# Feed-forwards: two 256-column products that share a weight become one of 512 columns

## The chip, the cores and the metric

One core of one Trainium2 chip runs the whole program. The metric is the device time of one execution in microseconds (us). Five engines work from queues of their own and meet at semaphores: TensorE (PE in the profile, its weight loads PEld), VectorE (DVE), ScalarE (ACT), GpSimd (POOL) and SyncE (SP), which here issues the loads of the weights.

## The reference

Three blocks in sequence act on 256 tokens of width 1024. Each has feed-forwards of width 2816 or other wide layers, and between them stand different mixers (attention, a convolution, a product-key memory). Eight feed-forwards of one kind are what the change touches:

```
def _swiglu(x, w_gate, w_up, w_down):
    return (jax.nn.silu(x @ w_gate) * (x @ w_up)) @ w_down
...
x = x + 0.5 * _swiglu(_rmsnorm(x, ffn1_norm[l]), ffn1_w_gate[l], ffn1_w_up[l], ffn1_w_down[l])
```

All of it is in fp32, with inputs and weights in fp32.

## The kernel before

**Two parts of each number.** A weight and an input are each held as a high part, rounded to the format fp32r, and a low part, the rest of the subtraction, in fp32r too. A product of the two is made of three matmuls into the same PSUM columns, in `product`: high weight by high input (L655), high weight by low input (L656), low weight by high input (L657). Each of them has 128 x 128 weights and 256 columns (the tokens), and each loads its weights itself: the high weight is loaded twice.

**Slabs.** Weights come in slabs of 1 MB (128 partitions x 2048 numbers), 16 products each, in one order for the whole program. SyncE loads slab m into a ring of 4 buffers, when slab m-4 has been used (`slab_done`). ScalarE's `round_slab` copies it to one of 3 buffers of high parts (L1427), when slab m-3 has been used, since that slab lies in the same buffer. VectorE's `rest_slab` subtracts (L1916) and puts the low part over the slab itself. Then `slab_rest` lets TensorE begin it. In all feed-forwards but their first steps ScalarE and VectorE have two slabs ready beyond the one on TensorE.

**A feed-forward** (`ffn` of the three engines) has 33 slabs. Slabs 0 to 21 are *ups*: up f gives 128 gate and 128 up columns of the hidden layer, in one of four pairs of PSUM banks (columns 0 to 255 of each bank; a bank holds 512). VectorE multiplies both by the norm's factor (`up_scaled`, L2015: PSUM to SBUF, 128x512), ScalarE applies Silu to the gate (L1509), VectorE multiplies gate and up (L2008), ScalarE copies the high part of the result (L1504) and VectorE subtracts for the low part (L2001). These five stand one tick apart: in tick t an engine rounds a slab, then does its later step for up t-2, then for t-1, then for t. Slabs 22 to 32 are *downs*, r = 0 to 10: each holds two of the 22 rows of weights, for 8 output chunks of 128 that gather in all 8 PSUM banks over all downs. In the last down (r = 10) the chunks end pair by pair, and VectorE adds half of each to x (L2028, `finish`) before the next stage takes its input from x.

At the start of a feed-forward, ups 0 and 1 run interleaved, TensorE sums the squares of x (L726, L727), and VectorE and ScalarE make the factor from the sums (a square root, then L1939, a reciprocal) before L2015 of up 0.

**Order.** Every engine's instructions stand in the order in which its `ffn` issues them. VectorE has, after its last tick, ten `rest_slab` in a row, then the adds to x. ScalarE has eleven `round_slab`. The tenth of VectorE's and of ScalarE's belongs to slab 33, the first of the next stage, which uses the buffer of high parts that slab 30 (down r = 8) holds.

## Time and profile before

| what | us |
|---|---|
| median of three runs | 4007.13 |
| lowest and highest of them | 4005.62, 4008.4 |
| span of the profiled execution, first to last instruction | 4004.4 |

The profiled execution's own device time is not listed apart from the three runs; they lie 1.2 to 4.0 us above its span, the median 2.7. TensorE is busy for 98% of the span, VectorE for 68%, ScalarE for 50%. How to read it: a matmul's duration (276 ns) is the time from its start to its modelled end, and matmuls overlap; what one costs is the distance from one start to the next. "PEclk" is the granted clock of TensorE as a share of 2.4 GHz; 0.50 is 1.2 GHz.

### The profile page before, as it was taken

What the parts mean: (1) busy time and instruction counts of PE and PEld (TensorE: products, weight loads), DVE (VectorE), ACT (ScalarE), POOL (GpSimd) and SP (SyncE); (2) the same over time, 40 slices, a digit from 0 to 9 for tenths busy, and PEclk for the clock granted to TensorE, in tenths of its full rate; (3) what the DMA queues carried; (4) which work ended last, traced back from release to release, by engine and by line L of the source; (5) the groups of instructions that cost most, each with busy time, mean ns of one, the idle gap of its engine ahead of it and who ended that gap; (6) DMA issues with size and microseconds to landing.
All of it is one profiled execution on the core that took longest, in us unless ns stands there. A gap on an engine that the chain in (4) does not pass through costs nothing.

```text
span 4004.4 us, 78708 instructions
## 1 busy us (share of the span) xinstructions
PE 3909.7 (98%) x34150; PEld 3793.3 (95%) x34150; DVE 2736.3 (68%) x4071; ACT 1987.8 (50%) x2620; POOL 212.2 (5%) x277
## 2 busy tenths in 40 slices
PE   8999999999999999999999999999999999999999
PEld 8979999889998999999997999999998899999999
DVE  6566665666655656567555799956756699974855
ACT  5445444454544545465435545754444544764443
POOL 0011000110002000010023000000000000000000
PEclk9999999999999999999998999999999999999999
DMA  6534555345555455534550455456654455455754
GB/s 237 192 115 151 192 190 190 133 148 195 181 194 182 160 199 184 195 133 173 191 204 34 159 194 181 177 199 233 229 196 153 158 177 193 175 182 202 265 199 158
DMA packets 114791, 720.78 MB, mean 180 GB/s; under 512 B 13328, under 2 KB 13664, under 8 KB 32784
## 3 DMA queue, kind: packets, MB, share of 16 engines
q1 hardware_dynamic: 90144, 652.25, 45.9%
q10 hardware_dynamic: 19200, 37.01, 2.5%
q0 software_dynamic: 5104, 26.49, 1.9%
q8 instruction: 270, 4.42, 0.4%
q14 instruction: 73, 0.60, 0.0%
HBM read 692.48 MB, written 23.22 MB: 179 GB/s over the span
## 4 chain that ended last, share of the span: by engine, by line
PE 87%; DVE 7%; ACT 4%; issue 1%; POOL 0%; DMA 0%; ACTq 0%; DVEq 0%; POOLq 0%
PE psum L655 26%; PE psum L657 26%; PE psum L656 26%; PE psum L1408 3%; DVE slab_low L1916 2%; ACT slab_high L1427 2%; DVE h_parts L2219 1%; PE psum L1065 1%; PE psum L1048 1%; PE psum L875 1%; PE psum L1078 1%; ACT room L1670 1%; DVE room L2248 0%; DVE room L2253 0%; PE psum L1349 0%
## 5 line engine op out<-in xcount | busy, mean ns | idle before, releaser
L1916 DVE TENSOR_TENSOR slab_low<-slab,slab_high 128x2048 fp32r<-128x2048 f32 x622 | 1423.2, 2289 | 738.8 <-ACT slab_high L1427 736.6
L655 PE MATMUL psum<-h_parts,slab_high 128*128 128x256 f32 x5632 | 1578.2, 280 | 28.9 <-DVE h_parts L2219 18.6
L1427 ACT ACTIVATE slab_high<-slab 128x2048 fp32r<-128x2048 f32 x622 | 1189.3, 1912 | 785.4 <-PE psum L657 721.1
L656 PE MATMUL psum<-h_parts,slab_high 128*128 128x256 f32 x5632 | 1556.5, 276 | 0.0
L657 PE MATMUL psum<-h_parts,slab_low 128*128 128x256 f32 x5632 | 1556.1, 276 | 0.0
L655 PEld LDWEIGHTS psum<-h_parts,slab_high 128*128 128x128 f32 x5632 | 1063.5, 189 | 48.8 <-issue 24.0
L655 PE MATMUL psum<-hidden_parts,slab_high 128*128 128x256 f32 x3840 | 1063.5, 277 | 11.4 <-DVE hidden_parts L2166 4.8
L656 PEld LDWEIGHTS psum<-h_parts,slab_high 128*128 128x128 f32 x5632 | 1063.5, 189 | 2.4 <-issue 2.2
L657 PEld LDWEIGHTS psum<-h_parts,slab_low 128*128 128x128 f32 x5632 | 1062.8, 189 | 0.0
L656 PE MATMUL psum<-hidden_parts,slab_high 128*128 128x256 f32 x3840 | 1058.0, 276 | 0.0
L657 PE MATMUL psum<-hidden_parts,slab_low 128*128 128x256 f32 x3840 | 1058.0, 276 | 0.0
L655 PEld LDWEIGHTS psum<-hidden_parts,slab_high 128*128 128x128 f32 x3840 | 722.0, 188 | 21.6 <-issue 12.9
L656 PEld LDWEIGHTS psum<-hidden_parts,slab_high 128*128 128x128 f32 x3840 | 722.2, 188 | 0.0
L657 PEld LDWEIGHTS psum<-hidden_parts,slab_low 128*128 128x128 f32 x3840 | 722.0, 188 | 0.0
L1889 ACT ACTIVATE hidden_parts<-room 128x512 fp32r<-128x512 f32 x128 | 80.9, 632 | 303.7 <-PE psum L657 294.7
L1880 ACT ACTIVATE room<-psum 128x512 f32<-128x512 f32 x128 | 76.5, 598 | 283.1 <-PE psum L657 283.1
L2598 DVE TENSOR_TENSOR hidden_parts<-room,hidden_parts 128x512 fp32r<-128x512 f32 x128 | 88.2, 690 | 135.1 <-ACT hidden_parts L1889 134.9
L2015 DVE TENSOR_TENSOR room<-psum,room 128x512 f32<-128x512 f32 x176 | 121.3, 689 | 62.8 <-PE psum L657 61.7
L2569 DVE TENSOR_SCALAR room<-consts,room 128x128 f32<-128x128 f32 x512 | 136.4, 339 | 0.0
L1408 PE MATMUL psum<-room 128*128 128x128 f32 x1024 | 124.5, 275 | 0.0
L1670 ACT ACTIVATE room<-room 128x128 f32<-128x128 f32 (+1 forms) x160 | 71.4, 448 | 105.6 <-DVE room L2253 78.6
L1408 PEld LDWEIGHTS psum<-room 128*128 128x128 f32 x1024 | 119.4, 191 | 0.0
(346 smaller groups left out, 3326.0 us busy)
## 6 DMA issues: line engine op xcount, KB each, us to landing
slab<-in_up SPq DMA_DIRECT2D x176, 1024.0 KB, 4.8
slab<-in_keys_up SPq DMA_DIRECT2D x128, 1024.0 KB, 4.8
slab<-in_keys_down SPq DMA_DIRECT2D x128, 1024.0 KB, 4.8
slab<-in_down SPq DMA_DIRECT2D x88, 1024.0 KB, 4.8
slab<-in_w_in SPq DMA_DIRECT2D x16, 1024.0 KB, 4.8
slab<-in_wq SPq DMA_DIRECT2D x16, 1024.0 KB, 4.8
peer_gates<-room ACTq DMA_DIRECT2D x64, 256.0 KB, 2.3
room<-peer_gates ACTq DMA_DIRECT2D x64, 256.0 KB, 5.4
```

Source lines behind the costliest of these rows:

```text
L655: nc.tensor.matmul(out, lhs[0], rhs[0], start=first, stop=False, **options)
L656: nc.tensor.matmul(out, lhs[0], rhs[1], start=False, stop=False, **options)
L657: return nc.tensor.matmul(out, lhs[1], rhs[0], start=False, stop=last, **options)
L1408: mm = nc.tensor.matmul(bank[:, t, :], v.firsts[:, b % 2, t, :], v.seconds[b % 2][:, t, :], start=True, stop=True)
L1427: nc.scalar.activation(k.high[m % PARTS][:, 0:width], k.slabs[m % RING][:, 0:width], ACT.Copy).then_inc(k.rounded.up())
L1670: ex = nc.scalar.activation(row, row, ACT.Exp, bias=small[:, e:e + 1], accum_out=small[:, 4 + e:5 + e])
L1880: nc.scalar.activation(v.hidden[:, at:at + 2, :], k.banks[4 + r % 2].rearrange("p (e t) -> p e t", e=2), ACT.Gelu_apprx_tanh).then_inc(k.a ...
L1889: nc.scalar.activation(k.hidden[:, at:at + 2, 0, :], v.hidden[:, place:place + 2, :], ACT.Copy).then_inc(k.hidden_rounded.up())
L1916: nc.vector.tensor_tensor(k.low[m % RING][:, 0:width], k.slabs[m % RING][:, 0:width], k.high[m % PARTS][:, 0:width], ALU.subtract).then_in ...
L2015: nc.vector.tensor_tensor(both, k.bank_pairs[(f + k.first_pair) % 4][:, :, 0:T], v.rstd.unsqueeze(1).to_broadcast([P, 2, T]), ALU.mult).th ...
L2569: hot = nc.vector.tensor_scalar(v.seconds[b % 2][:, t, :], iota, v.slots[:, 1, t0 + t:t0 + t + 1], v.slots[:, 2, t0 + t:t0 + t + 1], ALU.i ...
L2598: nc.vector.tensor_tensor(k.hidden[:, at:at + 2, 1, :], v.hidden[:, place:place + 2, :], k.hidden[:, at:at + 2, 0, :], ALU.subtract).then_ ...
```

## The change

An up's product now consists of two matmuls (`wide_product`): high weight by both input parts, which lie next to each other, 512 columns into a whole PSUM bank; and low weight by high input, 256 columns into its first half. The second half then holds the sums with the low input part, which has to be added by another engine. In an up ScalarE copies the second halves of the pair to SBUF and VectorE adds the first halves to them (`up_summed`); the scaling by the norm's factor is then an instruction of its own, SBUF to SBUF. In downs r = 0 to 8 the products are wide as well; after r = 8 VectorE adds half of each second half to x (four instructions, `lows_added`), and r = 9 and 10 use the three-matmul product into the first halves. Down r = 8 works four chunks at a time, and down r = 9 waits for the add of a pair of banks before it first writes that pair.

```diff
+WIDE_DOWNS = 9
...
+    def wide_product(self, bank, lhs, rhs, first, last):
+        nc = self.k.nc
+        nc.tensor.matmul(bank, lhs[0], rhs, start=first, stop=last, skip_group_check=True)
+        return nc.tensor.matmul(bank[:, 0:T], lhs[1], rhs[:, 0, :], start=False, stop=last, skip_group_check=True)
...
             if f >= 4:
-                nc.tensor.wait_ge(k.up_scaled.sem, k.up_scaled.at(f - 3))
+                nc.tensor.wait_ge(k.up_summed.sem, k.up_summed.at(f - 3))
...
             if f >= 2:
                 for a in range(2):
                     for c in range(DC):
-                        mm = self.product(pair[:, a], [part[:, a, c, :] for part in w], (k.h[:, c, 0, :], k.h[:, c, 1, :]), c == 0, c == DC - 1)
+                        mm = self.wide_product(pair[:, a], [part[:, a, c, :] for part in w], k.h[:, c], c == 0, c == DC - 1)
...
+            if r >= WIDE_DOWNS - 1:
+                nc.tensor.wait_ge(k.hidden_ready.sem, k.hidden_ready.at(2 * r + 2))
+                for half, e, n in itertools.product(range(2), range(2), range(DC // 2)):
+                    c, f = 4 * half + n, 2 * r + e
+                    cols = slice(e * D + c * P, e * D + (c + 1) * P)
+                    if r == WIDE_DOWNS - 1:
+                        mm = self.wide_product(k.banks[c], (high[:, cols], low[:, cols]), k.hidden[:, f], False, e == 1)
+                        if half == 0 and e == 1 and n == DC // 2 - 1:
+                            mm.then_inc(k.lows_done.up())
+                        continue
+                    if r == WIDE_DOWNS and e == 0 and n % 2 == 0:
+                        nc.tensor.wait_ge(k.lows_added.sem, k.lows_added.at(c // 2 + 1))
+                    mm = self.product(k.banks[c][:, 0:T], (high[:, cols], low[:, cols]), (k.hidden[:, f, 0, :], k.hidden[:, f, 1, :]), False, False, skip_group_check=True)
...
+            if tick < FC:
+                f = tick
+                nc.scalar.wait_ge(k.slab_done.sem, k.slab_done.at(f + 1))
+                nc.scalar.activation(v.both[:, f % 2], k.bank_pairs[(f + k.first_pair) % 4][:, :, T:2 * T], ACT.Copy).then_inc(k.up_copied.up())
...
-                nc.vector.wait_ge(k.slab_done.sem, k.slab_done.at(f + 1))
-                if f >= 2:
-                    nc.vector.wait_ge(k.multiplied.sem, k.multiplied.at(f - 1))
-                nc.vector.tensor_tensor(both, k.bank_pairs[(f + k.first_pair) % 4][:, :, 0:T], v.rstd.unsqueeze(1).to_broadcast([P, 2, T]),
-                                        ALU.mult).then_inc(k.up_scaled.up())
+                nc.vector.wait_ge(k.up_copied.sem, k.up_copied.at(f + 1))
+                nc.vector.tensor_tensor(both, k.bank_pairs[(f + k.first_pair) % 4][:, :, 0:T], both, ALU.add).then_inc(k.up_summed.up())
+                nc.vector.wait_ge(k.up_summed.sem, k.up_summed.at(f + 1))
+                nc.vector.tensor_tensor(both, both, v.rstd.unsqueeze(1).to_broadcast([P, 2, T]), ALU.mult).then_inc(k.up_scaled.up())
         for r in range(FC // 2 - 1):
             self.rest_slab()
+        for j in range(DC // 2):
+            if j == 0:
+                nc.vector.wait_ge(k.lows_done.sem, k.lows_done.at(1))
+            if j == 2:
+                nc.vector.wait_ge(k.slab_done.sem, k.slab_done.at(FC + WIDE_DOWNS))
+            both = k.x[:, 2 * j:2 * j + 2, :]
+            nc.vector.scalar_tensor_tensor(out=both, in0=k.bank_pairs[j][:, :, T:2 * T], scalar=0.5, in1=both,
+                                           op0=ALU.mult, op1=ALU.add).then_inc(k.lows_added.up())
```

On TensorE, where the first feed-forward passes from down r = 8 (its last row in `slab_high0`) to r = 9 (`slab_high1`), before the change:

```order
L655 MATMUL psum<-hidden_parts_66,slab_high0_57 128x256
L656 MATMUL psum<-hidden_parts_66,slab_high0_57 128x256
L657 MATMUL psum<-hidden_parts_66,slab_low2_55 128x256
L655 MATMUL psum<-hidden_parts_66,slab_high1_58 128x256 [waits hidden_ready,slab_rest]
L656 MATMUL psum<-hidden_parts_66,slab_high1_58 128x256
L657 MATMUL psum<-hidden_parts_66,slab_low3_56 128x256
```

The same place after the change:

```order
L664 MATMUL psum<-hidden_parts_66,slab_high0_57 128x512
L665 MATMUL psum<-hidden_parts_66,slab_low2_55 128x256
L657 MATMUL psum<-hidden_parts_66,slab_high1_58 128x256 [waits lows_added,hidden_ready,slab_rest]
L658 MATMUL psum<-hidden_parts_66,slab_high1_58 128x256
L659 MATMUL psum<-hidden_parts_66,slab_low3_56 128x256
```

A product of down r = 8 has two matmuls in place of three, and the first matmul of r = 9 waits for `lows_added` too.

On VectorE, at the end of the same feed-forward (the last two of its ten `rest_slab`, slabs 32 and 33, and what follows; x is the running sum, `h_parts` the next stage's input), before the change:

```order
L1916 TENSOR_TENSOR slab_low0_53<-slab0_49,slab_high2_59 128x2048 [waits slab_rounded]
L1916 TENSOR_TENSOR slab_low1_54<-slab1_50,slab_high0_57 128x2048 [waits slab_rounded]
L2028 SCALAR_TENSOR_TENSOR x_63<-psum,x_63 128x512 [waits pair_done] x2
L2219 SCALAR_TENSOR_TENSOR h_parts_60<-x_63,vectors_61,h_parts_60 128x256 [waits h_rounded] x2
L2028 SCALAR_TENSOR_TENSOR x_63<-psum,x_63 128x512 [waits pair_done]
```

The same place after the change:

```order
L1942 TENSOR_TENSOR slab_low0_53<-slab0_49,slab_high2_59 128x2048 [waits slab_rounded]
L1942 TENSOR_TENSOR slab_low1_54<-slab1_50,slab_high0_57 128x2048 [waits slab_rounded]
L2050 SCALAR_TENSOR_TENSOR x_63<-psum,x_63 128x512 [waits lows_done]
L2050 SCALAR_TENSOR_TENSOR x_63<-psum,x_63 128x512
L2050 SCALAR_TENSOR_TENSOR x_63<-psum,x_63 128x512 [waits slab_done]
L2050 SCALAR_TENSOR_TENSOR x_63<-psum,x_63 128x512
L2062 SCALAR_TENSOR_TENSOR x_63<-psum,x_63 128x512 [waits pair_done,lows_added]
```

The four new adds (L2050) stand behind the low part of slab 33, whose high part goes into the buffer that r = 8 reads.

On VectorE, one tick in the midst of the first feed-forward's ups, before the change:

```order
L1916 TENSOR_TENSOR slab_low2_55<-slab2_51,slab_high1_58 128x2048 [waits slab_rounded]
L2001 TENSOR_TENSOR hidden_parts_66<-room_65,hidden_parts_66 128x256 [waits hidden_rounded]
L2008 TENSOR_TENSOR room_65<-room_65 128x256 [waits hidden_ready,gated]
L2015 TENSOR_TENSOR room_65<-psum,room_65 128x512 [waits multiplied,slab_done]
L1916 TENSOR_TENSOR slab_low3_56<-slab3_52,slab_high2_59 128x2048 [waits slab_rounded]
```

A tick after the change:

```order
L1942 TENSOR_TENSOR slab_low1_54<-slab1_50,slab_high0_57 128x2048 [waits slab_rounded]
L2027 TENSOR_TENSOR hidden_parts_66<-room_65,hidden_parts_66 128x256 [waits hidden_rounded]
L2034 TENSOR_TENSOR room_65<-room_65 128x256 [waits hidden_ready,gated]
L2039 TENSOR_TENSOR room_65<-psum,room_65 128x512 [waits up_copied]
L2041 TENSOR_TENSOR room_65<-room_65 128x512 [waits up_summed]
L1942 TENSOR_TENSOR slab_low2_55<-slab2_51,slab_high1_58 128x2048 [waits slab_rounded]
```

One instruction over PSUM has become one over PSUM that waits for ScalarE, and one over SBUF.

## Rows read from the trace of the kernel before

**Rows 1.** The page: busy time of each engine; shares of the last-ending chain.

```profile
PE 3909.7 (98%) x34150; PEld 3793.3 (95%) x34150; DVE 2736.3 (68%) x4071; ACT 1987.8 (50%) x2620; POOL 212.2 (5%) x277
PE 87%; DVE 7%; ACT 4%; issue 1%; POOL 0%; DMA 0%; ACTq 0%; DVEq 0%; POOLq 0%
```

**Rows 2.** Timeline, ScalarE, late downs of feed-forward 1: start us, us, instruction [idle before].

```profile
182.26 1.92 ACT L1427 ACTIVATE slab_high<-slab 128x2048 fp32r<-128x2048 f32 x1 [3.52 <-PE psum L657]
187.70 1.92 ACT L1427 ACTIVATE slab_high<-slab 128x2048 fp32r<-128x2048 f32 x1 [3.52 <-PE psum L657]
```

**Rows 3.** Timeline, TensorE in an up: the first and last of 28 matmuls.

```profile
59.95 0.28 PE L655 MATMUL psum<-h_parts,slab_high 128*128 128x256 f32 x1
...
63.01 0.28 PE L655 MATMUL psum<-h_parts,slab_high 128*128 128x256 f32 x1
```

**Rows 4.** Timeline, TensorE, matmuls of 128 columns: first and last of ten.

```profile
227.35 0.27 PE L657 MATMUL psum<-slab_high,h_parts 128*128 128x128 f32 x1
...
228.35 0.28 PE L657 MATMUL psum<-slab_high,h_parts 128*128 128x128 f32 x1
```

**Rows 5.** Timeline, TensorE, plain fp32: first and thirteenth of 256 columns; one of 512.

```profile
2012.17 0.59 PE L1180 MATMUL psum<-room 128*128 128x256 f32 x2
...
2017.36 0.59 PE L1180 MATMUL psum<-room 128*128 128x256 f32 x2
...
2092.89 1.02 PE L1235 MATMUL psum<-room,consts 128*128 128x512 f32 x2
2093.74 0.51 PE L1256 MATMUL psum<-consts,room 128*128 128x16 f32 x4
```

**Rows 6.** Groups by line and form: ScalarE from PSUM, VectorE within SBUF (count | busy, mean ns).

```profile
L1880 ACT ACTIVATE room<-psum 128x512 f32<-128x512 f32 x128 | 76.5, 598 | 283.1 <-PE psum L657 283.1
L2598 DVE TENSOR_TENSOR hidden_parts<-room,hidden_parts 128x512 fp32r<-128x512 f32 x128 | 88.2, 690 | 135.1 <-ACT hidden_parts L1889 134.9
```

**Rows 7.** Timeline, VectorE and ScalarE, a tick in the ups.

```profile
105.16 0.42 DVE L2008 TENSOR_TENSOR room<-room 128x256 f32<-128x256 f32 x1
106.05 0.69 DVE L2015 TENSOR_TENSOR room<-psum,room 128x512 f32<-128x512 f32 x1 [0.46 <-PE psum L657]
108.06 2.29 DVE L1916 TENSOR_TENSOR slab_low<-slab,slab_high 128x2048 fp32r<-128x2048 f32 x1 [1.32 <-ACT slab_high L1427]
...
106.10 1.92 ACT L1427 ACTIVATE slab_high<-slab 128x2048 fp32r<-128x2048 f32 x1 [2.91 <-PE psum L657]
```

**Rows 8.** Timeline, VectorE and TensorE, start of feed-forward 6.

```profile
1345.56 1.75 DVE L1939 RECIPROCAL room<-room 128x256 f32<-128x256 f32 x1 [0.48 <-ACT room L1451]
1347.34 0.69 DVE L2015 TENSOR_TENSOR room<-psum,room 128x512 f32<-128x512 f32 x1
1347.95 2.28 DVE L1916 TENSOR_TENSOR slab_low<-slab,slab_high 128x2048 fp32r<-128x2048 f32 x1
...
1350.29 0.39 PE L655 MATMUL psum<-h_parts,slab_high 128*128 128x256 f32 x1 [0.20 <-DVE slab_low L1916]
```

**Rows 9.** Timeline, VectorE, late downs of feed-forward 1 (the tenth low part, then x).

```profile
189.66 2.29 DVE L1916 TENSOR_TENSOR slab_low<-slab,slab_high 128x2048 fp32r<-128x2048 f32 x1 [3.15 <-ACT slab_high L1427]
194.44 0.69 DVE L2028 SCALAR_TENSOR_TENSOR x<-psum,x 128x512 f32<-128x512 f32 x1 [2.49 <-PE psum L657]
```

**Rows 10.** Windows of 2 us around TensorE's longest late wait: us, PE, PEld, DVE, ACT, POOL, PEclk, DMA.

```profile
1302.00:1304.00 2.00, 0.28 (x2) 0.00 (x0) 1.20 (x2) 1.21 (x2) 0.00 (x0) 1.00 0.00 0
1304.00:1306.00 2.00, 0.00 (x0) 0.00 (x0) 1.74 (x3) 1.02 (x2) 0.00 (x0) 0.83 0.00 0
1310.00:1312.00 2.00, 2.00 (x12) 2.00 (x11) 0.00 (x0) 0.00 (x0) 0.00 (x0) 0.50 0.00 0
```

**Rows 11.** Timeline, TensorE behind two waits: first matmul and first at full pace.

```profile
1307.12 0.55 PE L655 MATMUL psum<-hidden_parts,slab_high 128*128 128x256 f32 x1 [4.84 <-DVE hidden_parts L2166]
...
1312.17 0.28 PE L657 MATMUL psum<-hidden_parts,slab_low 128*128 128x256 f32 x1
...
3069.74 0.38 PE L655 MATMUL psum<-h_parts,slab_high 128*128 128x256 f32 x1
...
3073.50 0.28 PE L655 MATMUL psum<-h_parts,slab_high 128*128 128x256 f32 x1
```

More of the change, by code:

```diff
@@ L231, in __init__ @@
         self.up_scaled, self.gated, self.multiplied = signal("up_scaled"), signal("gated"), signal("multiplied")
+        self.up_copied, self.up_summed, self.lows_added, self.lows_done = (signal(n) for n in ("up_copied", "up_summed", "lows_added", "lows_done"))
         self.pair_done = signal("pair_done")
@@ L691, in ffn @@
             at = (f + k.first_pair) % 4
-            pair = k.bank_pairs[at][:, :, 0:T]
+            pair = k.bank_pairs[at]
             if f >= 4:
-                nc.tensor.wait_ge(k.up_scaled.sem, k.up_scaled.at(f - 3))
+                nc.tensor.wait_ge(k.up_summed.sem, k.up_summed.at(f - 3))
             elif f >= 2 or k.first_pair < 2:
@@ L703, in ffn @@
                 firsts, lag = [], FIRST_LAG if first else DC if k.before == "ffn" else 2
-                pairs = [k.bank_pairs[g + k.first_pair][:, :, 0:T] for g in range(2)]
+                pairs = [k.bank_pairs[g + k.first_pair] for g in range(2)]
                 for step in range(DC + lag):
@@ L714, in ffn @@
                         for a in range(2):
-                            mm = self.product(pairs[g][:, a], [part[:, a, c, :] for part in firsts[g]], (k.h[:, c, 0, :], k.h[:, c, 1, :]), c == 0, c == DC - 1)
+                            mm = self.wide_product(pairs[g][:, a], [part[:, a, c, :] for part in firsts[g]], k.h[:, c], c == 0, c == DC - 1)
                         if c == DC - 1:
@@ L733, in ffn @@
             if f == 5 and first:
-                nc.tensor.wait_ge(k.up_scaled.sem, k.up_scaled.at(4))
+                nc.tensor.wait_ge(k.up_summed.sem, k.up_summed.at(4))
                 self.bias_lines()
@@ L742, in ffn @@
                     mm = self.product(k.banks[2 * j + c][:, 0:T], (high[:, cols], low[:, cols]),
-                                      (k.hidden[:, 2 * r + e, 0, :], k.hidden[:, 2 * r + e, 1, :]), False, e == 1)
+                                      (k.hidden[:, 2 * r + e, 0, :], k.hidden[:, 2 * r + e, 1, :]), False, e == 1, skip_group_check=True)
                     if e == 1 and c == 1 and j < 3:
@@ L747, in ffn @@
                 break
+            if r >= WIDE_DOWNS - 1:
[11 more added lines that the diff above has]
+                    mm = self.product(k.banks[c][:, 0:T], (high[:, cols], low[:, cols]), (k.hidden[:, f, 0, :], k.hidden[:, f, 1, :]), False, False, skip_group_check=True)
+                mm.then_inc(k.slab_done.up())
+                continue
             for e in range(2):
@@ L754, in ffn @@
                     if f == 0 and n % 2 == 0:
-                        nc.tensor.wait_ge(k.up_scaled.sem, k.up_scaled.at(FC - 3 + n // 2))
+                        nc.tensor.wait_ge(k.up_summed.sem, k.up_summed.at(FC - 3 + n // 2))
                     cols = slice(e * D + c * P, e * D + (c + 1) * P)
-                    mm = self.product(k.banks[c][:, 0:T], (high[:, cols], low[:, cols]), (k.hidden[:, f, 0, :], k.hidden[:, f, 1, :]),
-                                      f == 0, False)
+                    mm = self.wide_product(k.banks[c], (high[:, cols], low[:, cols]), k.hidden[:, f], f == 0, False)
             mm.then_inc(k.slab_done.up())
@@ L2011, in ffn @@
                 both = v.both[:, f % 2]
[L2012 to L2016 removed]
+                nc.vector.wait_ge(k.up_copied.sem, k.up_copied.at(f + 1))
+                nc.vector.tensor_tensor(both, k.bank_pairs[(f + k.first_pair) % 4][:, :, 0:T], both, ALU.add).then_inc(k.up_summed.up())
+                nc.vector.wait_ge(k.up_summed.sem, k.up_summed.at(f + 1))
+                nc.vector.tensor_tensor(both, both, v.rstd.unsqueeze(1).to_broadcast([P, 2, T]), ALU.mult).then_inc(k.up_scaled.up())
         for r in range(FC // 2 - 1):
             self.rest_slab()
+        for j in range(DC // 2):
[6 more added lines that the diff above has]
+                                           op0=ALU.mult, op1=ALU.add).then_inc(k.lows_added.up())
         self.owed = True
+        nc.vector.wait_ge(k.lows_added.sem, k.lows_added.at(DC // 2))
         pair_done, all_done = [k.pair_done.at(j + 1) for j in range(3)], k.slab_done.at(FC + FC // 2)
```

## Prediction

> **What bounds the kernel now.** I began with the page's busy times and its chain of waits: TensorE is busy for 98% of the span and holds 87% of the chain [rows 1], so the question is what one product costs on TensorE, and whether anything new makes it wait. The busy share does not answer the first, since matmul durations overlap; the pace does. In the downs, ScalarE starts a slab each time TensorE has finished one, at 182.26 and 187.70: 5.44 us for a slab of 48 matmuls, 113.3 ns each [rows 2]. I went through these starts in the ups and downs of all eight feed-forwards: nearly every distance is 5.44. Single starts agree: 27 distances in 3.06 us are 113.3 ns [rows 3]. A product of three is 340.0 ns.
>
> What makes up the 113.3? With 128 columns, half the streaming, nine distances take 1.00 us: 111.1 ns [rows 4]. So columns are not what sets it there; each of these matmuls loads 128 x 128 weights, and I read 111 ns as the least distance between two loads. Streaming alone shows in plain fp32. There twelve steps of 256 columns take 5.19 us, 432.5 ns a step, and a step of 512 columns takes 0.85 us, twice that [rows 5]; each step has two records, and 432.5 is four times 108.1, so I read four passes of 256 / 2.4 GHz = 106.7 ns with little on top. The matmuls of the feed-forward thus lie where the two limits meet: 107 to 108 ns of streaming, 111 of loading, 113.3 together.
>
> **TensorE's gain.** A wide product has one matmul of 512 columns and one of 256, two loads in place of three. The load for the second lies beside 213.3 ns of streaming and is hidden; the load for the next product lies beside 256 columns as now. So it costs 512 columns at the pace of the fp32 passes, 2 x 108.1 = 216.2, plus 113.3, together 329.5; with a load per matmul I allow half a nanosecond more and take 330, a gain of 10.0 ns. The bounds: if the 6.6 ns above streaming come with each matmul (113.3 - 106.7), one of them is saved, 6.7 ns; if nothing but streaming counted, the product would take 213.3 + 107.5 = 320.8, a gain of 19.2. I choose near the fp32 rows since they show 512 columns without a surcharge. There are 8 x (22 + 9) x 16 = 3968 wide products: **-39.7 us** (bounds -26.6 and -76.2).
>
> The Trainium skill, in TensorE: Matmul & The Clock Gate, section Back-to-back issue gap, gives an isolated matmul of N columns N / 2.4 + 2.5 ns. By that a product would fall from 327.5 to 325.0 only, 9.9 us in all, and the sum below would be 4061.6. The row has 113.3 where this formula has 109.2, so it leaves out the load; the sum goes by the rows.
>
> **The ups' extra work, at nothing.** Per up ScalarE gets a PSUM copy of 128x512, 0.60 us by its like, and VectorE one more pass over 128x512 in SBUF, 0.69 by its like [rows 6]. Call the end of a slab 0, as ScalarE and VectorE see it in [rows 7] (106.10, 106.05). Now: copy to 0.65, rounding of the next slab to 2.55; VectorE adds to 1.3, scales to 1.95, idles until 2.55, makes the low part to 4.8, then its two steps of 0.35 to 5.5. The next slab ends at 16 x 0.330 = 5.28, its copy at 5.93: VectorE still waits some 0.4 us in each tick. And the low part so made is for the slab after the next two, needed 5.5 us later than it is done. A bank pair comes free 0.6 us later than now, three slabs ahead of its use; for the first down's last pair, whose adding ends 1.6 us into 1.98 us of other products, 0.4 us is left. What hides all this is VectorE's idle time; if a tick were longer than the slab, each 0.1 us would cost 176 x 0.1 = 17.6 us.
>
> **The start of a feed-forward.** Here VectorE has no idle time. The reciprocal ends at 1347.31, L2015 of up 0 follows at 1347.34, the low part at 1347.95, and TensorE waits for it until 1350.29 [rows 8]. The copy on ScalarE hides beside the reciprocal, but the scaling now puts 0.6 us ahead of the low part; and the 16 products that TensorE runs meanwhile end 0.16 us sooner. I found such a wait in seven of the eight feed-forwards: 7 x 0.76 = 5.3, with a little for the eighth **+6 us** (3 to 9).
>
> **The new wait at down 9.** TensorE may not begin r = 9 before VectorE has added the first pair's low halves. On VectorE that add stands behind the low part of slab 33, this behind ScalarE's rounding of slab 33, and this waits until slab 30, which is r = 8 itself, is done. So none of the chain can run beside r = 8. Its length stands in the trace: ScalarE starts at 187.70 [rows 2], VectorE's low part at 189.66, 1.96 later; it takes 2.29, of which the next instruction waits 2.21; an add of x from PSUM takes 0.69 [rows 9]. That is 4.86 us from ScalarE's start. TensorE's next start would have been 0.26 before it (187.44 in the timeline), and the restart costs about 0.05 and a load of 0.12: 5.3 us of nothing on TensorE. Behind it the second pair's add comes 0.6 later, in time for TensorE. Nothing is paid back: slabs 31 and 32 were ready anyway, and the next stage waits for x, which is late by the same. Eight times: **+42.4 us**.
>
> **The clock behind the wait.** After the wait of 4.84 us the granted clock had fallen from 1.00 to 0.50, 1.2 GHz, while TensorE was idle, and stayed there [rows 10]. Matmuls then stand 213 ns apart; from the restart at 1307.12 to the first at full pace at 1312.17 there are 23, in 5.05 us where 2.61 would have done: 2.44 lost. A shorter break ended in 18 at this pace, 3.76 us for 2.04: 1.72 lost [rows 11]. I take 2.0: 8 x 2.0 = **+16.0 us** (0 if it stayed up, 19 at the longer). The Trainium skill, same page, section Why this matters for your kernels, warns that idle gaps between bursts of matmuls send the array back to half rate; by that rule the change pays beyond its idle time, and the trace agrees, with 0.50 at 1310.
>
> **Sum.** 4004.4 (the profiled span) - 39.7 + 6 + 42.4 + 16.0 = 4029.1; the median of the runs lies 2.7 above that span, so **4031.8**, 0.6% slower.
>
> **The rivals.**
> *Streaming only (faster).* If the second load too can be hidden beside the 512 columns, the gain is 76.2: 3995.3. For it: both loads, 222 ns, are shorter than the stream. Against: 113.3 lies above both limits, so a load does not start before its predecessor's matmul. Costs of 64.4 us over 3968 products make 16.2 ns the gain from which the change is faster.
> *The clock holds.* Terms as above without 16.0: 4015.8. Against: in [rows 10] it fell during a shorter wait than the new one.
> *Nothing is saved.* If the surplus grows with the columns (226.6 + 113.3 = 340), only costs are left, 42.4 + 16.0 + 4.2 (the scaling alone at the seven starts): 4069.7. Against: 512 fp32 columns at exactly twice 256.
> *VectorE becomes the bound in the ups.* A tick of 5.4 us in place of 5.28 would give 21 us more, 4053. Against: 0.4 us of room.
>
> **How the numbers follow.** The forecast has 0.68, nothing saved 0.09, the clock holds 0.08, VectorE bound 0.08, streaming only 0.07. The forecast's own range: at a gain of 13 ns (51.6), a start of 3 and stalls of 6.6 each, 4011; at 6.7 ns, 9 and 7.6, 4050. That leaves out about 2 in 10 with the cases beyond, so 4010 to 4052 is the range. What a measurement can tell from no change is about 0.2%, 8 us: faster means below 3999 (streaming only, and a rest: 0.08), same up to 4015 (half of the clock's case and the forecast's low end: 0.12), slower 0.80.
>
> **What the profile would show.** Right: slabs every 5.28 us in the ups; before each r = 9 an idle TensorE of about 5 us, released by VectorE's L2050, and a clock of 0.50 behind it; VectorE idle before L2039 in the ups. Wrong: a slab time of 5.44 (nothing saved) or 5.13 (streaming only); waits of TensorE for `up_summed` or low parts in the middle of the ups (VectorE bound); or r = 9 starting within a microsecond of r = 8, which would mean that I misread the order on VectorE.

## The result, and the profile after

The changed kernel takes 4120.01 us (median of four runs, 4119.01 to 4121.45), the kernel before 4006.38 beside it (4004.87 to 4008.4): a ratio of 1.0281, 95% interval 1.0267 to 1.0296. It is 114 us slower; 25 were predicted. The profiled execution has a span of 4118.8 us, 114.4 more than before.

The page, busy times and chain, to be read against [rows 1]:

```profile
PE 3976.0 (97%) x30182; PEld 3673.8 (89%) x30182; DVE 2875.2 (70%) x4279; ACT 2073.3 (50%) x2796; POOL 215.5 (5%) x277
PE 86%; DVE 8%; ACT 4%; issue 1%; DMA 0%; POOL 0%; ACTq 0%; DVEq 0%; POOLq 0%
```

TensorE has 3968 instructions fewer and is busy 66 us longer. Its pace, in the timeline of the changed kernel in an up, a wide product and the first of the next:

```profile
80.24 0.40 PE L664 MATMUL psum<-h_parts,slab_high 128*128 128x512 f32 x1
80.48 0.28 PE L665 MATMUL psum<-h_parts,slab_low 128*128 128x256 f32 x1
80.60 0.40 PE L664 MATMUL psum<-h_parts,slab_high 128*128 128x512 f32 x1
```

From one wide product to the next is 0.36 us: the 512 columns take 0.24 and the 256 behind them 0.12 (medians over all the ups 235 and 118 ns). The slabs say it more finely, as in [rows 2]; the timeline of ScalarE in the changed kernel, the first and the fourth of four starts:

```profile
81.65 1.91 ACT L1449 ACTIVATE slab_high<-slab 128x2048 fp32r<-128x2048 f32 x1
...
98.61 1.91 ACT L1449 ACTIVATE slab_high<-slab 128x2048 fp32r<-128x2048 f32 x1
```

16.96 us for three slabs, 5.65 each where 5.28 was forecast, are 353.3 ns a product, where three matmuls took 340.0: a loss of 13.3 ns, 3968 times, **52.8 us**, instead of a gain of 39.7.

The wait at down 9. First the changed kernel's groups of waits (us in total, times, longest), then its timelines of VectorE and TensorE in feed-forward 1:

```profile
PE psum L657 <- DVE x L2050: 41.4, 8, 5.8
```

```profile
196.22 2.29 DVE L1942 TENSOR_TENSOR slab_low<-slab,slab_high 128x2048 fp32r<-128x2048 f32 x1 [3.35 <-ACT slab_high L1449]
198.43 2.48 DVE L2050 SCALAR_TENSOR_TENSOR x<-psum,x 128x512 f32<-128x512 f32 x4
...
199.26 0.55 PE L657 MATMUL psum<-hidden_parts,slab_high 128*128 128x256 f32 x1 [5.08 <-DVE x L2050]
```

Eight waits, 41.4 us in all. And the clock behind this one (windows of 2 us, columns as in [rows 10]):

```profile
194.00:196.00 2.00, 0.18 (x2) 0.00 (x0) 0.00 (x0) 1.72 (x1) 0.00 (x0) 1.00 0.36 57
196.00:198.00 2.00, 0.00 (x0) 0.00 (x0) 1.78 (x1) 0.19 (x1) 0.00 (x0) 0.75 0.92 381
198.00:200.00 2.00, 0.74 (x3) 0.77 (x4) 2.00 (x4) 0.00 (x0) 0.00 (x0) 0.50 0.21 86
...
204.00:206.00 2.00, 2.00 (x20) 2.00 (x19) 0.00 (x0) 0.00 (x0) 0.00 (x0) 1.00 0.00 0
```

The granted clock falls to 0.50 in the wait and stays there for 3.1 to 5.9 us behind each of the eight restarts. Counted as at [rows 11], the matmuls up to the first at full pace lost 1.49 to 2.84 us a time, 18.0 in all. The terms read so far come to 52.8 + 41.4 + 18.0 = 112.2. The starts of the feed-forwards come on top: in seven of them TensorE's wait for the low part, 0.20 us before [rows 8], is 0.76 now. The timeline of the changed kernel, start of feed-forward 6:

```profile
1421.40 0.50 PE L664 MATMUL psum<-h_parts,slab_high 128*128 128x512 f32 x1 [0.76 <-DVE slab_low L1942]
```

All waits of TensorE for low parts went from 10.0 to 13.7 us. With these 3.7 the terms make 115.9, 1.5 more than the 114.4 by which the span grew.

### The profile page after: what moved, and what is told of

Read it like the earlier page. It is cut to its first block, busy times and chain, and to the rows that moved or that the text cites. A ratio compares the mean times of both kernels' runs of the same rounds, so it can differ in the third digit from the quotient of the medians.

```text
span 4118.8 us, 71002 instructions
## 1 busy us (share of the span) xinstructions
PE 3976.0 (97%) x30182; PEld 3673.8 (89%) x30182; DVE 2875.2 (70%) x4279; ACT 2073.3 (50%) x2796; POOL 215.5 (5%) x277
## 4 chain that ended last, share of the span: by engine, by line
PE 86%; DVE 8%; ACT 4%; issue 1%; DMA 0%; POOL 0%; ACTq 0%; DVEq 0%; POOLq 0%
PE psum L664 21%; PE psum L657 15%; PE psum L658 15%; PE psum L659 15%; PE psum L665 11%; PE psum L1430 3%; DVE slab_low L1942 3%; ACT slab_high L1449 2%; DVE h_parts L2253 1%; PE psum L1087 1%; PE psum L1070 1%; PE psum L897 1%; PE psum L1100 1%; ACT room L1696 1%; DVE room L2282 0%
## 5 line engine op out<-in xcount | busy, mean ns | idle before, releaser
L664 PE MATMUL psum<-h_parts,slab_high 128*128 128x512 f32 x2816 | 1001.4, 399 | 27.1 <-DVE h_parts L2253 17.0
L657 PE MATMUL psum<-hidden_parts,slab_high 128*128 128x256 f32 x2688 | 755.7, 281 | 52.8 <-DVE x L2050 41.4
L657 PE MATMUL psum<-h_parts,slab_high 128*128 128x256 f32 x2816 | 797.0, 283 | 8.1 <-DVE h_parts L2253 4.3
L665 PE MATMUL psum<-h_parts,slab_low 128*128 128x256 f32 x2816 | 793.3, 282 | 0.0
L658 PE MATMUL psum<-h_parts,slab_high 128*128 128x256 f32 x2816 | 780.0, 277 | 0.0
L659 PE MATMUL psum<-h_parts,slab_low 128*128 128x256 f32 x2816 | 779.7, 277 | 0.0
L658 PE MATMUL psum<-hidden_parts,slab_high 128*128 128x256 f32 x2688 | 748.9, 279 | 0.0
L659 PE MATMUL psum<-hidden_parts,slab_low 128*128 128x256 f32 x2688 | 748.5, 278 | 0.0
L664 PEld LDWEIGHTS psum<-h_parts,slab_high 128*128 128x128 f32 x2816 | 529.8, 188 | 162.4 <-issue 14.3
L657 PEld LDWEIGHTS psum<-hidden_parts,slab_high 128*128 128x128 f32 x2688 | 513.8, 191 | 65.3 <-DVE slab_low L1942 48.5
L657 PEld LDWEIGHTS psum<-h_parts,slab_high 128*128 128x128 f32 x2816 | 532.8, 189 | 23.1 <-issue 10.9
L658 PEld LDWEIGHTS psum<-h_parts,slab_high 128*128 128x128 f32 x2816 | 533.0, 189 | 2.2 <-issue 2.2
L658 PEld LDWEIGHTS psum<-hidden_parts,slab_high 128*128 128x128 f32 x2688 | 513.9, 191 | 0.0
L659 PEld LDWEIGHTS psum<-hidden_parts,slab_low 128*128 128x128 f32 x2688 | 513.4, 191 | 0.0
L664 PE MATMUL psum<-hidden_parts,slab_high 128*128 128x512 f32 x1152 | 407.4, 397 | 0.0
L665 PE MATMUL psum<-hidden_parts,slab_low 128*128 128x256 f32 x1152 | 324.3, 281 | 0.0
L1535 ACT ACTIVATE room<-psum 128x512 f32<-128x512 f32 x176 | 104.8, 596 | 357.0 <-PE psum L665 356.8
L664 PEld LDWEIGHTS psum<-hidden_parts,slab_high 128*128 128x128 f32 x1152 | 216.4, 188 | 53.2
```

Of the source, the lines that this page charges most:

```text
L657: nc.tensor.matmul(out, lhs[0], rhs[0], start=first, stop=False, **options)
L658: nc.tensor.matmul(out, lhs[0], rhs[1], start=False, stop=False, **options)
L659: return nc.tensor.matmul(out, lhs[1], rhs[0], start=False, stop=last, **options)
L664: nc.tensor.matmul(bank, lhs[0], rhs, start=first, stop=last, skip_group_check=True)
L665: return nc.tensor.matmul(bank[:, 0:T], lhs[1], rhs[:, 0, :], start=False, stop=last, skip_group_check=True)
L1535: nc.scalar.activation(v.both[:, f % 2], k.bank_pairs[(f + k.first_pair) % 4][:, :, T:2 * T], ACT.Copy).then_inc(k.up_copied.up())
```

## The experiments

**The wait alone.** The four adds of low halves stand ahead of VectorE's low part of slab 33 (run e2_adds_first):

```diff
-        for r in range(FC // 2 - 1):
+        for r in range(FC // 2 - 2):
             self.rest_slab()
         for j in range(DC // 2):
...
+        self.rest_slab()
```

> One line of order differs from the changed kernel: on VectorE the four adds of the low halves (after down 8) stand ahead of the tenth low part (slab 33, first slab of the next stage) and not behind it. Theory (the add waits behind a low part that waits for down 8 itself): the eight waits of 5.08 us before down 9 go, and with them the half clock behind them, whose losses add up to 18 us in the trace after: 42 + 18 = 60 us less, about 4060. Rival (the wait is only moved to where the next stage needs slab 33, since its low part is later by the four adds): TensorE waits there instead, and the time falls by less than 20, 4100 or more.

4060.13 us; 4008.57 before it; ratio 1.0128 (1.0111 to 1.0145). That is 59.9 less than the changed kernel (62.1, if each is taken against the kernel before beside it), where wait and clock had been read as 41.4 + 18.0 = 59.4. The same window of this run, and VectorE's timeline:

```profile
196.00:198.00 2.00, 2.00 (x20) 2.00 (x19) 1.76 (x1) 0.20 (x1) 0.00 (x0) 1.00 0.93 389
```

```profile
192.79 1.28 DVE L2050 SCALAR_TENSOR_TENSOR x<-psum,x 128x512 f32<-128x512 f32 x2
194.22 1.29 DVE L2050 SCALAR_TENSOR_TENSOR x<-psum,x 128x512 f32<-128x512 f32 x2 [0.16 <-PE psum L665]
196.24 2.29 DVE L1942 TENSOR_TENSOR slab_low<-slab,slab_high 128x2048 fp32r<-128x2048 f32 x1 [0.72 <-ACT slab_high L1449]
```

The adds fit where VectorE had waited for ScalarE, the low part starts when it did, TensorE does not stop and the clock stays at 1.00. Half of the loss was the place of four instructions. The other half remains, and is on TensorE.

**Which part of the rest.** Three runs, each with one part of the change: only the downs wide (with the adds as above), only the ups wide, and the kernel before with only the ups' extra copy and pass on ScalarE and VectorE.

```diff
# e4_downs_alone, ups, against e2_adds_first (ScalarE's copy and VectorE's add go too)
-    mm = self.wide_product(pair[:, a], ..., k.h[:, c], c == 0, c == DC - 1)
+    mm = self.product(pair[:, a], ..., (k.h[:, c, 0, :], k.h[:, c, 1, :]), c == 0, c == DC - 1)
# e5_ups_alone, downs, against the changed kernel (the adds of low halves go too)
-    mm = self.wide_product(k.banks[c], ..., k.hidden[:, f], f == 0, False)
+    mm = self.product(k.banks[c][:, 0:T], ..., (k.hidden[:, f, 0, :], k.hidden[:, f, 1, :]), f == 0, False)
# e6_ups_work, against e5_ups_alone: ups of product() as well, and
-    nc.scalar.activation(v.both[:, f % 2], k.bank_pairs[...][:, :, T:2 * T], ACT.Copy)
+    nc.scalar.activation(v.both[:, f % 2], k.bank_pairs[...][:, :, 0:T], ACT.Copy)
-    nc.vector.tensor_tensor(both, k.bank_pairs[...][:, :, 0:T], both, ALU.add)
+    nc.vector.tensor_tensor(both, k.bank_pairs[...][:, :, 0:T], both, ALU.max)
```

> The changed kernel with its ups as they were before (products of three matmuls, no copy and no add of low halves) and only its downs 0 to 8 wide; the low halves are added to x ahead of VectorE's low part of slab 33, as in the run of that name, so that TensorE does not wait at r = 9. Theory: a wide product costs 353.3 ns against 340.0 in the downs too, 8 x 9 x 16 = 1152 of them, 15.3 us over the kernel before (about 4007), so 4020 to 4025. If the predicted gain of 10 ns held here and the loss belonged to the ups (to the address of h_parts, or to VectorE's and ScalarE's extra work beside the matmuls), it would be 4007 - 11.5 = 3996; if the downs were neutral, 4007.

> The changed kernel with its downs as they were before (three matmuls a product, nothing to add at the end), only the ups wide, with ScalarE's copy and VectorE's add. Theory: 8 x 22 x 16 = 2816 wide products at 13.3 ns more are 37.5 us, and the start of seven feed-forwards waits 0.7 to 0.8 us longer, 5.3: 4007 + 43 = 4050 (4045 to 4053). If the wide product gained 10 ns as predicted and all was lost in the downs: 4007 - 28.2 + 5.3 = 3984. No fall of the clock is expected in the middle of a feed-forward.

> The kernel before, all products of three matmuls, with only the ups' extra work of ScalarE and VectorE: ScalarE copies the high half of each up from PSUM (in place of the low half), VectorE takes the maximum of the two, which is the same number, and scales from SBUF. It prices this work without any change on TensorE. As predicted: nothing in the middle of the ups, and 7 x 0.76 us at the starts of the feed-forwards, so 4007 + 5 = 4010 to 4014. Rival (the work slows the ups by itself, by a tick longer than a slab of 5.44 us or by holding up TensorE's memory): 0.1 us a tick would be 17.6 us, so 4025 or more. If the starts cost nothing, 4007.

Beside 4004.85 us for the kernel before, the downs alone take 4022.12 (1.0043, 1.0028 to 1.0057), the ups alone 4046.16 (1.0099, 1.0082 to 1.0116), the ups' extra work alone 4011.93 (1.0019, 1.0009 to 1.0028). So the extra work costs 7.1 us. TensorE's groups of waits show it at the starts, before and in e6_ups_work:

```profile
PE psum L655 <- DVE slab_low L1916: 10.0, 16, 1.2
...
PE psum L657 <- DVE slab_low L1928: 16.9, 17, 2.0
```

And the wide product loses in the ups, (41.3 - 7.1) / 2816 = 12.1 ns, as in the downs, 17.3 / 1152 = 15.0, whatever ScalarE and VectorE do beside it. The intervals leave about 3 and 5 ns to either side, so the 13.3 read from the slabs fits both.

**The pace by itself.** Two runs, each executed once, compute nothing of the blocks; TensorE runs series of fp32r matmuls, nearly all with new weights for each (e3_paces_by_address: 16 or 32 each):

```diff
+for mov in moves:                       # e1_paces: twelve addresses of the moving part
+    mm(bank[0][:, 0:T], w(high, i), m(mov, i)[:, 0:T], ...)    # and two more: of three
+    mm(bank[1], w(high, i), m(mov, i), ...)                    # 512, then 256: wide
...
+r = run(390, 128, 240, 512, 32)         # e3_paces_by_address: address of weights, of moving part, columns, count
+for i in range(r['n']):
+    last = mm(r['o'], r['w'][i], r['m'][i], start=i == 0, stop=i == r['n'] - 1, ...)
```

> Nothing of the three blocks is computed; the program rounds x to a high and a low part as weights, and TensorE runs series of 16 products over them, so that each series has one pace to read. For each of twelve start addresses of the moving input (remainder modulo 512 bytes: 240 as in the kernel, then 0, 16, 64, 112, 128, 176, 256, 304, 368, 432, 496) there are three series: the product of three matmuls of 256 columns, the wide product (512 and 256), and 512 columns alone with a new weight each time. Theory A (columns): each column costs 0.46 ns whatever the address, so 512 alone takes 235 ns at every address, 384 columns 177, 320 columns 147, and the wide product 353. Theory B (address): the 235 ns of the 512 columns come from where the input lies against the weights; some of the twelve addresses give 216 to 220 ns for 512 and 330 for the wide product, others more than 353. Theory C (bank): the 512 waits for or blocks the matmul of 256 into the same bank; with that one in another bank the wide product falls to 330, and 512 alone takes 216 at all addresses. Theory D (load): the weight load beside a matmul slows it; 512 columns with the same weight still load each time, so they tell nothing apart from A, but 256 columns at 113 and 128 at 111 say what a load costs alone.

> Nothing of the blocks is computed: TensorE alone runs fp32r matmuls, each with its own 128 x 128 weights, in series of 16 or 32, each series on its own line. The first run of this kind showed 233 to 237 ns for a matmul of 512 columns at twelve addresses of the moving part, all with weights that begin on a multiple of 512 bytes, and 113 to 120 for 256. In the kernel the weights begin 128 bytes behind such a multiple and the moving parts 240 behind. Here: six addresses of the weights by 32 of the moving part, 512 and 256 columns each; then seven widths, smaller weights (64 and 32 columns), half the rows, bf16 and plain fp32. Theory A (each load of weights holds the stream up, wherever the operands lie): 512 columns take 230 to 237 ns at every pair of addresses; with weights of 32 columns, a load of a quarter, they fall to under 220; at widths above 300 the surplus over columns / 2.4 GHz is a constant 17 to 20 ns. Theory B (the addresses collide): at some pair of addresses 512 columns take 213 to 220 while 256 take 113, so that a wide product takes 326 to 333 there, as predicted; at the kernel's pair it is 235. Theory C (reading fp32r is slow by column): the surplus grows in proportion to the columns, smaller weights change nothing, and bf16 at 512 columns takes 213 to 217.

In e1_paces 512 columns took 230 to 235 ns alone at twelve addresses, 226 to 237 as the first half of a wide product, and 234 with the second half in another bank, so neither the address nor the shared bank alone makes the 235. In e3_paces_by_address the range over 192 pairs of addresses is 227 to 236, and 114 to 120 for 256 columns. The widths and kinds are in its timeline; the pace is the distance of two starts over 32 (plain fp32 has two records a matmul):

```profile
1117.06 3.85 PE L1216 MATMUL psum<-moving,weights 128*128 128x256 f32 x32
1120.75 4.86 PE L1219 MATMUL psum<-moving,weights 128*128 128x320 f32 x32
1125.44 5.71 PE L1222 MATMUL psum<-moving,weights 128*128 128x384 f32 x32
1130.99 6.76 PE L1225 MATMUL psum<-moving,weights 128*128 128x448 f32 x32
1137.59 7.56 PE L1228 MATMUL psum<-moving,weights 128*128 128x512 f32 x32
1144.98 7.56 PE L1231 MATMUL psum<-moving,weights 128*64 128x512 f32 x32
...
1178.32 7.08 PE L1249 MATMUL psum<-moving,weights 128*128 128x512 bf16 x32
1185.24 3.66 PE L1252 MATMUL psum<-moving,weights 128*128 128x256 bf16 x32
1188.73 27.63 PE L1255 MATMUL psum<-xs 128*128 128x512 f32 x64
1216.20 13.98 PE L1258 MATMUL psum<-xs 128*128 128x256 f32 x64
```

115.3 ns at 256 columns, 173.4 at 384, 230.9 at 512: close to a straight line of 0.45 ns a column, where bf16 has 216.3 for 512 and plain fp32 858.4 / 4 = 214.6 a pass. Weights of a quarter of the columns save 4 ns (226.9). So Theory C of that run stands in the main: most of the cost lies with the moving columns, not with the loads.

**What in the columns.** e7_order_and_steps runs whole products in the kernel's order at 32 addresses of the moving part and four of the weights, and then 512 columns read in other steps (one execution).

```diff
+        last = go(bank[2], part(weights, 128, i), cols(240, i, 0, 1).to_broadcast([P, 512]), i == 0, i == 31)
...
+        last = go(bank[4], part(weights, 128, i), moving[:, 60:60 + 512].rearrange('p (a t) -> p t a', a=2), i == 0, i == 31)
```

> Nothing of the blocks is computed. The run on addresses gave 227 to 236 ns for 512 fp32r columns at 192 pairs of addresses, 113 to 121 for 256, a straight line over the widths (115.3 at 256, 173.4 at 384, 230.9 at 512: 0.45 ns a column), 226.9 with weights of 32 columns, but 216.3 and 109.1 in bf16 and 214.6 for each of fp32's four passes over 512. So the surplus of fp32r goes by column and not by load (Theory C). This run asks what in the column it is, and whether any address helps the kernel's own order of matmuls. (1) Whole products in the kernel's order, with high and low weights from two tensors, wide and of three, at 32 addresses of the moving part by four of the weights. If the addresses decide between wide and three, somewhere the wide one takes under 335 ns; by the paces so far no place gives under 341, and the three take 340 at the best. (2) 512 fp32r columns read in other steps: one column over and over (512 or 256 times), eight columns 64 times, every second column, the two halves interleaved; and weights that repeat one column. If the reading of new data from memory holds the stream up, a column read over and over takes 213 to 218 ns for 512; if fp32r itself streams slower than a column in 0.417 ns, it stays at 230 to 235. bf16 with every second column (the same span of memory) stays at 216 if the bytes read count, and rises to 230 if the span does.

Its timeline, weights at 128 as in the kernel: 16 wide products with the moving part at 224, 16 of three, then both at 240; then, at 1478.72, 512 columns in order, one column 512 times, every second column, the two halves in turn (1507.52), and eight columns 64 times. Each row is where a series begins:

```profile
193.72 0.40 PE L54 MATMUL psum<-moving,weights 128*128 128x512 f32 x1
...
199.32 0.40 PE L54 MATMUL psum<-moving,weights 128*128 128x256 f32 x2
...
205.08 0.39 PE L54 MATMUL psum<-moving,weights 128*128 128x512 f32 x1
...
210.73 0.40 PE L54 MATMUL psum<-moving,weights 128*128 128x256 f32 x2
...
216.19 0.39 PE L54 MATMUL psum<-moving,weights 128*128 128x512 f32 x1
...
1478.72 7.55 PE L54 MATMUL psum<-moving,weights 128*128 128x512 f32 x32
1486.12 7.07 PE L54 MATMUL psum<-moving,weights 128*128 128x512 f32 x32
1493.02 14.68 PE L54 MATMUL psum<-moving,weights 128*128 128x512 f32 x32
1507.52 7.09 PE L54 MATMUL psum<-moving,weights 128*128 128x512 f32 x32
1514.44 7.13 PE L54 MATMUL psum<-moving,weights 128*128 128x512 f32 x32
```

At 240, the kernel's address, a wide product takes 353 ns and one of three 341, as in the kernel. At 224 it is 350 and 360. Over all 128 pairs of addresses products of three range from 340 to 360 and wide ones from 343 to 353. So the address decides which is faster: the wide one is, by over 1 ns, at 108 of the 128, but 240, with the weights at 128 as in the kernel, is among the best for three and among the worst for wide. No address brings the wide one near the 330 of the prediction. In order, 512 columns take 231; one column over and over, 215.8; the halves in turn, 216.4; eight neighbouring columns 64 times, 218. Weights that repeat one column leave the 512 columns in order at 235, so what is slow is not the reading of the weights. And bf16, 216 in order, takes 226 with every second column.

**The address in the kernel.** `RESIDUE` is that address: 224 in place of 240, once in the kernel before and once in e2_adds_first.

```diff
-RESIDUE = 240
+RESIDUE = 224
```

> The kernel before with one number changed: the moving parts (h_parts, early_parts and hidden_parts) begin 224 bytes behind a multiple of 512 instead of 240. Measured by themselves, at this address a product of three takes 359.6 ns instead of 341.6 and a wide one 350.4 instead of 353.1. If the addresses set the pace in the kernel as they do there, the slab in ups and downs goes from 5.44 to 5.74 us; all 9728 products of 256 columns give 4005 + 175 = 4180 if the mixers are bound by TensorE as well, the 4224 of the feed-forwards alone 4081: so 4081 to 4180, nearer to the upper end. Rival (113.3 ns is what the loads of weights allow, as the prediction had it): nothing changes, 4005.

> The changed kernel with the low halves added ahead of the low part of slab 33 (no wait at r = 9), at the same other address, 224. At 240 this version takes 55 us more than the kernel before. By the paces measured alone, the wide products cost 350.4 ns here against 359.6 for three: 3968 x 9.2 = 36 us less than the kernel before at 224, and 5 more for the starts, so about 30 us FASTER than that one (the run beside it), whatever the mixers do. Rival (a wide product costs more than three matmuls wherever they lie, as something of its own): 50 to 60 us slower than that one, as at 240.

The kernel before takes 4180.24 us at 224 (1.0432, 1.0415 to 1.0450), 173 more than at 240, where 175 were expected if the mixers slow down with the feed-forwards; the changed one takes 4144.13 (1.0341, 1.0324 to 1.0358): **36 us faster** than its neighbour, where it was 52 slower at 240 (4060.13 against 4008.57). ScalarE's slab starts in the two at 224, 5.76 and 5.60 us apart, 360 and 350 ns a product:

```profile
81.58 1.92 ACT L1427 ACTIVATE slab_high<-slab 128x2048 fp32r<-128x2048 f32 x1 [2.80 <-PE psum L657]
87.34 1.92 ACT L1427 ACTIVATE slab_high<-slab 128x2048 fp32r<-128x2048 f32 x1 [3.23 <-PE psum L657]
```

```profile
81.37 1.91 ACT L1449 ACTIVATE slab_high<-slab 128x2048 fp32r<-128x2048 f32 x1
86.97 1.91 ACT L1449 ACTIVATE slab_high<-slab 128x2048 fp32r<-128x2048 f32 x1
```

**The order of the columns.** e8_reading_orders (one execution) measures strides and whole products; e11 and e12 read each part's two halves in turn in the feed-forwards, one of the two fastest orders.

```diff
# matmuls, of e2_adds_first (e11_change_in_turn) and of the kernel before (e12_before_in_turn)
-    nc.tensor.matmul(bank, lhs[0], rhs, ...)
+    nc.tensor.matmul(bank, lhs[0], rhs.rearrange("p b (a t) -> p b t a", a=2), ...)
-    (k.hidden[:, f, 0, :], k.hidden[:, f, 1, :])
+    (in_turn(k.hidden[:, f, 0, :]), in_turn(k.hidden[:, f, 1, :]))      # "p (a t) -> p t a"
# where PSUM is read
+    back(pair)                                                          # "p e (t a) -> p e a t"
```

> Nothing of the blocks is computed. The run before showed 512 fp32r columns at 231 ns when they are read one after the other, at 215.8 when one column is read 512 times, and at 216.4 when the two halves are read in turn (columns 0, 256, 1, 257, ...): so it is the order in which memory is read that holds the stream up. Here the same in other orders, weights 128 and moving parts 240 bytes behind a multiple of 512: strides of 8 to 256 columns over 512 or 256 columns, the two halves apart each read in a permuted order of its own (what the kernel could use, since the results then lie in the same permuted order in both), and whole products, wide and of three, in these orders at five addresses. If any large stride avoids the collision, 512 take 214 to 218 ns and 256 take 109 to 112 for all of them, a wide product 325 to 330 and one of three 328 to 334, at all five addresses alike. If only the distance of 256 columns (1024 bytes) does it, the permuted halves stay at 229 to 236 and 113 to 120, and the products as they were: 353 and 342 at 240.

> The changed kernel with the low halves added ahead of the low part of slab 33, and in the feed-forwards the columns of each moving part read in turn from its two halves (0, 128, 1, 129, ...), two matmuls a product as in the change; VectorE and ScalarE undo the order where they read PSUM (the last adds to x in two pieces a pair for it). By the paces measured alone a wide product takes 327.3 ns so, against 353.6 in order: 3968 x 26 = 103 us off the 4060 of the version that it is built on, and about 3 more at the starts, where the faster products wait for the same low part: 3955 to 3965, faster than the kernel before by 1.0 to 1.3%. A slab in the ups every 5.24 us. Rival (VectorE or ScalarE read the permuted PSUM columns more slowly and become the bound in the ups, where VectorE has some 0.3 us of room a tick): 17.6 us for each 0.1 us beyond it, 3980 to 4020. Rival (the loss of the wide product is not the order of the columns): 4060.

> The kernel before, three matmuls a product as ever, with the same order of reading in the feed-forwards. By the paces measured alone a product of three takes 335.0 ns so, at any address, against 340 to 342 at the address it has: 4224 products of the feed-forwards, 21 to 28 us less than the kernel before, 3978 to 3986; a slab every 5.36 us. The difference to the changed kernel in the same order is then what the change itself is worth where no reading order or address disturbs it: 335.0 - 327.3 = 7.7 ns for 3968 products, 30.6 us, less the 8 of the starts, 20 to 25 us in favour of the change. Rival (the reading of permuted PSUM columns costs VectorE time that shows): nothing gained or slower, 4007 or more.

The timeline of e8_reading_orders: 512 columns in order, with the halves in turn, in quarters, in eighths, and (L73) each part's halves in turn; then 16 wide products and 16 of three in that last order at 240, up to 217.01:

```profile
34.85 7.56 PE L59 MATMUL psum<-moving,weights 128*128 128x512 f32 x32
42.25 7.07 PE L61 MATMUL psum<-moving,weights 128*128 128x512 f32 x32
49.15 8.91 PE L63 MATMUL psum<-moving,weights 128*128 128x512 f32 x32
57.90 15.78 PE L65 MATMUL psum<-moving,weights 128*128 128x512 f32 x32
...
115.16 7.09 PE L73 MATMUL psum<-moving,weights 128*128 128x512 f32 x32
...
206.41 0.38 PE L102 MATMUL psum<-moving,weights 128*128 128x512 f32 x1
...
211.65 0.28 PE L105 MATMUL psum<-moving,weights 128*128 128x256 f32 x1
...
217.01 0.45 PE L109 MATMUL psum<-moving,weights 128*128 128x512 f32 x1
```

Wide 327, three 335, and so at all five addresses (327.2 to 327.4; 335.0). Only halves help: quarters take 273 ns, eighths 487. In the kernels: e11_change_in_turn 3969.45 us (0.9914, 0.9897 to 0.9930), **faster than the kernel before**, by 0.9%; e12_before_in_turn 3996.37 (0.9968, 0.9956 to 0.9981); 4004.64 before. Slab starts on ScalarE in e11_change_in_turn:

```profile
83.14 1.90 ACT L1463 ACTIVATE slab_high<-slab 128x2048 fp32r<-128x2048 f32 x1
88.38 1.91 ACT L1463 ACTIVATE slab_high<-slab 128x2048 fp32r<-128x2048 f32 x1
```

5.24 us, 327.5 ns a product; 5.36 in the other. In this order the change is worth 27 us by the medians, where 20 to 25 were expected; the lowest runs of the two lie 15 apart. Reading PSUM back in order costs VectorE nothing (689 ns a pass, as before). Both runs came out above what was expected, by 4 and 10 us. In the second, TensorE waits twice for GpSimd in the mixers, at places where the kernel before did not (groups of waits, e12_before_in_turn):

```profile
PE psum L1034 <- POOL room L2638: 5.9, 1, 5.9
PE psum L878 <- POOL room L2638: 3.7, 1, 3.7
```

The first has the like of the 3.7 only. What GpSimd is late for there was not tried, and some of the 27 us may be these waits; the second's ten runs spread from 3981.63 to 4001.56.

## Why the prediction was wrong

- **The step that failed is TensorE's gain**, -39.7 us as predicted, +52.8 measured: the sign was wrong, and with it the sum. The wide product was priced at 216.7 ns for its 512 columns and 113.3 for the 256 behind them; in the kernel they take 235 and 118. Two readings lay beneath it. The 113.3 ns were taken as loads of weights that meet 107 ns of streaming. The line over the widths, 115.3 at 256 columns and 0.45 for each one more, puts them down to the moving columns as well: a load alone would not grow with the columns. Below 256 the pace hardly falls (110.0 at 128), and 256 columns take 111.5 with the halves in turn: there the loads may bind, as the prediction said. And the pace of 512 columns was taken from plain fp32 [rows 5], which has no surcharge in order; fp32r has (230.9 against 214.6 a pass). Alike in width, the rows were not alike in type. The Trainium skill, in TensorE: Matmul & The Clock Gate, section Back-to-back issue gap, gives N / 2.4 + 2.5 ns for an isolated matmul, which is 215.8 and 109.2 ns: bf16 in order agrees (216.3 and 109.1), and so does fp32r with the halves in turn for 512 (215.8), but fp32r in order does not (230.9 and 115.3).
- The bounds were too narrow with it: -26.6 to -76.2 held no loss. Even the rival *nothing is saved* let the surplus grow only in proportion to the columns, 340 ns. Measured are 353.3: the address that gives three matmuls nearly their best pace (340, of 340 to 360) gives the wide product its worst (353, of 343 to 353). Why the 256 columns take 5 ns longer behind 512 was not tried.
- That the wide product of 330 exists was right, though not in this order of columns: 327.3 with the halves in turn, against 335.0 for three.
- **The wait at down 9** was right: 42.4 predicted, 41.4 in the groups of waits, by the chain on VectorE that was forecast; e2_adds_first shows that its cause is the place of the adds.
- **The clock** was right: 16.0 predicted, 18.0 read, and e2_adds_first gives 59.9 for wait and clock together against 58.4. The rival *the clock holds* fell in the windows.
- **The ups' extra work** costs nothing in the middle of the ups, as said, and **the starts** 7.1 us by themselves (e6_ups_work) against +6; in the changed kernel the waits for low parts grew by 3.7 only, and the 16 slower products ahead of each start hide 0.2 us more of it. The rival *VectorE becomes the bound* fell; with longer slabs it had more room than forecast, and at 5.24 us, in e11_change_in_turn, it still did not bind.
- *Streaming only* fell in every run: at best 327.

## What to carry to other kernels

A pace is carried from one width to another only within one type and one order of reading. Where the trace does not hold the very shape, a small run of that matmul alone at the kernel's own addresses gives it (353 and 341 ns here, against 353.3 and 340.0 in the kernels); until then the bounds of the gain must include a loss. A kernel whose data lie at an address that suits its own instructions can make a change look bad that is good elsewhere: compare at an address, or in an order, that favours neither. And before a new wait is paid for, look for an idle stretch ahead of it on the engine that is late: 60 us here went with four instructions moved ahead of one other.

## What was not expected of the hardware

The order in which fp32r columns are read from SBUF sets the pace of a matmul: 512 columns take 231 ns one after the other, 216 with columns 0 and 256 in turn (1024 bytes apart) or 0 and 128 (512 bytes), 273 in four places 512 bytes apart, 431 to 487 in eight or more, and 453 with every second column. Reading neighbours in order is not slow by itself: eight of them, read 64 times, take 218. The address counts too: a move of 16 bytes in where the moving parts begin made the whole kernel 4.3% slower. The Trainium skill, in SBUF — State Buffer, section Door 1: The DMA port swizzle, says that successive accesses run at full pace while they stay in a line of 16 bytes, and that each step into another line costs something. One column over and over agrees (215.8). The two halves in turn do not: they leave the line at every column and are as fast, and reading in order is slower. What in the memory causes this was not shown; neither half the rows (234.7) nor smaller weights (226.9) removed it, and bf16 in order did not have it (216.3).
